# Opening of a hybrid two-block transformer kernel: filler matmuls on zeros, x through a diagonal of roots, two weight slots issued ahead of the vectors

## The reference, cut to what matters

```python
h_res = concatenate([meta, x], axis=1)                       # 272 rows x 1024
h = h_res * rsqrt(mean(h_res * h_res) + 1e-6) * pre_norm_g   # row by row
z = h @ w_in                                                 # 1024 x 7328
```

## Time and profile before

| | us |
|---|---|
| median of 3 runs | 927.73 |
| lowest and highest | 925.45, 928.86 |
| the profiled execution, its own time | 930.4 |
| its span in the profile | 928.7 |
| PE busy | 891.5 (96% of the span) |
| DVE busy | 607.8 |
| ACT busy | 438.3 |

### The profile page before, as it was taken

The page is one execution under the profiler, slowest core; times in us unless marked ns, Lnnn a source line. Parts: engine busy times, 40 slices in busy tenths (PEclk is TensorE's granted clock), DMA queues, the critical chain, the costliest instruction groups (busy, mean ns, idle before and its releaser), DMA issues.

```text
span 928.7 us, 14251 instructions
## 1 busy us (share of the span) xinstructions
PE 891.5 (96%) x6011; PEld 816.0 (88%) x6011; DVE 607.8 (65%) x851; ACT 438.3 (47%) x606; POOL 120.8 (13%) x109
## 2 busy tenths in 40 slices
PE   6999989999999999989999999989999899999994
PEld 5997989998888888779999988779988899999883
DVE  5996994786568745785555544676886755555446
ACT  5555453555645853434444443234564444444430
POOL 0333430121002101020000000023600200000002
PEclk9999998999999999989999999989999999999998
DMA  8663664663347552546666555446634565555641
GB/s 300 188 175 95 187 190 126 180 181 114 92 136 231 177 161 77 172 137 185 187 188 187 185 183 187 155 156 193 191 116 138 171 189 184 182 181 182 188 152 46
DMA packets 117801, 154.20 MB, mean 166 GB/s; under 512 B 5263, under 2 KB 95786, under 8 KB 117706
## 3 DMA queue, kind: packets, MB, share of 16 engines
q1 hardware_dynamic: 116266, 148.31, 52.7%
q0 software_dynamic: 1472, 4.98, 1.6%
HBM read 151.44 MB, written 1.05 MB: 164 GB/s over the span
## 4 chain that ended last, share of the span: by engine, by line
PE 88%; DVE 9%; DMA 2%; ACT 1%; issue 0%; DVEq 0%; SPq 0%
PE acc L527 25%; PE acc L528 25%; PE acc L529 25%; PE acc L565 3%; DVE w_lo L1471 2%; DVE conv L1617 1%; DVE y L1901 1%; PE misc L653 1%; DVE rs L1501 1%; PE misc L717 1%; DVE rs L1505 1%; DMA x<-in_x 1%; ACT w_hi L1073 1%; PE misc L898 1%; DVE stats L1888 1%; DVE y L1876 0%
## 5 line engine op out<-in xcount | busy, mean ns | idle before, releaser
L1471 DVE TENSOR_TENSOR w_lo<-staged,w_hi 128x1024 fp32r<-128x1024 f32 x274 | 340.1, 1251 | 226.2 <-ACT w_hi L1073 225.7
L1073 ACT CAST w_hi<-staged 128x1024 fp32r<-128x1024 f32 x274 | 285.2, 1045 | 239.4 <-DMA staged<-in_ffn_w_gu 71.5
L527 PE MATMUL acc<-x_hi,w_hi 128*128 128x256 f32 (+1 forms) x1296 | 368.1, 284 | 3.1 <-DVE m L1696 3.1
L528 PE MATMUL acc<-x_lo,w_hi 128*128 128x256 f32 (+1 forms) x1296 | 367.4, 283 | 0.0
L529 PE MATMUL acc<-x_hi,w_lo 128*128 128x256 f32 (+1 forms) x1296 | 364.6, 281 | 0.0
L527 PEld LDWEIGHTS acc<-x_hi,w_hi 128*128 128x128 f32 x1296 | 244.3, 188 | 5.5 <-DVE m L1696 3.3
L529 PEld LDWEIGHTS acc<-x_hi,w_lo 128*128 128x128 f32 x1296 | 246.6, 190 | 0.0
L528 PEld LDWEIGHTS acc<-x_lo,w_hi 128*128 128x128 f32 x1296 | 244.9, 189 | 0.4 <-issue 0.2
L2257 POOL TENSOR_TENSOR y<-y,gain 128x512 f32<-128x512 f32 x8 | 10.4, 1306 | 461.0 <-ACT y L1269 461.0
L527 PE MATMUL acc<-w_hi,h_hi 128*128 128x512 f32 x176 | 69.7, 396 | 0.3 <-DVE hidden L2051 0.3
L529 PE MATMUL acc<-w_hi,h_lo 128*128 128x512 f32 x176 | 69.6, 396 | 0.0
(11 more groups left out here) (368 smaller groups left out, 1126.2 us busy)
## 6 DMA issues: line engine op xcount, KB each, us to landing
staged<-in_ffn_w_gu SPq DMA_DIRECT2D x88, 512.0 KB, 3.5
staged<-in_w_in SPq DMA_DIRECT2D x58, 512.0 KB, 3.7
staged<-in_ffn_w_down SPq DMA_DIRECT2D x44, 512.0 KB, 3.5
staged<-in_gla_w_in SPq DMA_DIRECT2D x24, 512.0 KB, 3.6
staged<-in_moba_w_in SPq DMA_DIRECT2D x24, 512.0 KB, 3.9
staged<-in_w_o SPq DMA_DIRECT2D x8, 512.0 KB, 3.7
staged<-in_gla_w_out SPq DMA_DIRECT2D x8, 512.0 KB, 3.6
staged<-in_moba_w_out SPq DMA_DIRECT2D x8, 512.0 KB, 3.6
```

Source lines behind the costliest of these rows:

```text
L527: pe.matmul(dst, st_hi, mv_hi, start=start, stop=False)
L528: pe.matmul(dst, st_hi, mv_lo, start=False, stop=False)
L1073: nc.scalar.copy(hi, raw).then_inc(rounded, 1)
L1471: nc.vector.tensor_tensor(lo, raw, hi, ALU.subtract).then_inc(split, 1)
```

## The change

- **PE on zeros.** PE no longer waits for the identity before its first matmul. It does 10 filler matmuls on `w_gk`, cleared to zero by POOL (that memset moves ahead of the one of `w_pool`), then 5 instead of 4 fillers with the identity, and 3 instead of 1 behind the vectors.
- **Diagonals.** Instead of scaling the rows (one ACT and two DVE instructions of 1024 columns) DVE multiplies the identity by the roots: three diagonal matrices of 128 columns, in the same buffer that y used. PE then multiplies x by the diagonal, as a float32 matmul, where it transposed the scaled rows. DVE waits for `const_loaded` in addition.
- **Order of loads.** Slots 0 and 1 are issued right behind x and ahead of the 11 vector loads; slots 2 and 3 behind them. The meta rows and the identity are issued by ACT. ACT squares the meta rows first, then tile 0.

```diff
@@ SP @@
-            sp.dma_start(m_rows, d["meta_tokens"]).then_inc(s["meta_loaded"], 16)
-            sp.dma_start(const[:, 0:2 * P], d["constants"][:, 0:2 * P]).then_inc(s["const_loaded"], 16)
+            z_slots(0, 2)
             for name, n in VEC_ROWS:
...
-            z_slots(0, 4)
+            z_slots(2, 4)
@@ PE @@
+            pe.wait_ge(s["cleared"], 2)
+            for _ in range(10):
+                pe.matmul(open_bank("vec")[:, 0:2 * P], w_gk[:, 0:P], w_gk[:, 0:2 * P], start=True, stop=True)
             pe.wait_ge(s["const_loaded"], 16)
-            keep_awake(open_bank("vec"), 4)
+            keep_awake(open_bank("vec"), 5)
             pe.wait_ge(s["vec_loaded"], 16 * len(VEC_ROWS))
             filled(pe.transpose(open_bank("vec")[:, 0:VEC_N], vec_rows[0:VEC_N, :], ident[0:VEC_N, 0:VEC_N]), "vec")
-            keep_awake(open_bank("x0_0"), 1)
+            keep_awake(open_bank("x0_0"), 3)
             pe.wait_ge(s["normed"], 3)
...
-                    pe.transpose(b[:, 0:META], meta_h[:, cols], ident[0:META, 0:META])
+                    pe.matmul(b[:, 0:META], m_rows[:, cols], diag(2)[0:META, 0:META], start=True, stop=True)
                     for t in range(TILES):
-                        tr = pe.transpose(b[:, META + t * P:META + t * P + P], y[:, t, cols], ident)
-                    filled(tr, "x0_%d" % c)
+                        mm = pe.matmul(b[:, META + t * P:META + t * P + P], x[:, t, cols], diag(t), start=True, stop=True)
+                    filled(mm, "x0_%d" % c)
@@ ACT @@
+            act.dma_start(m_rows, d["meta_tokens"]).then_inc(s["meta_loaded"], 16)
+            act.dma_start(const[:, 0:2 * P], d["constants"][:, 0:2 * P]).then_inc(s["const_loaded"], 16)
+            act.wait_ge(s["cleared"], 1)
+            act.wait_ge(s["meta_loaded"], 16)
+            nc.scalar.activation(meta_h, m_rows, ACT.Square, accum_out=ssq[0:META, 1:2])
             act.wait_ge(s["x_loaded"], 16)
-            act.wait_ge(s["cleared"], 1)
-            nc.scalar.activation(y[:, 0, :], x[:, 0, :], ACT.Square, accum_out=ssq[:, 0:1])
-            act.wait_ge(s["meta_loaded"], 16)
-            nc.scalar.activation(meta_h, m_rows, ACT.Square, accum_out=ssq[0:META, 1:2]).then_inc(s["ssq0"], 1)
-
-            act.wait_ge(s["rstd0"], 1)
-            nc.scalar.activation(y[:, 0, :], x[:, 0, :], ACT.Copy, scale=rs[:, 1, 0:1]).then_inc(s["normed"], 1)
+            nc.scalar.activation(y[:, 0, :], x[:, 0, :], ACT.Square, accum_out=ssq[:, 0:1]).then_inc(s["ssq0"], 1)
@@ DVE @@
-            nc.vector.tensor_scalar(y[:, 1, :], x[:, 1, :], rs[:, 1, 2:3], None, ALU.mult).then_inc(s["normed"], 1)
-            nc.vector.tensor_scalar(meta_h, m_rows, rs[0:META, 1, 1:2], None, ALU.mult).then_inc(s["normed"], 1)
+            dve.wait_ge(s["const_loaded"], 16)
+            for i, rows in ((2, META), (0, P), (1, P)):
+                of = (0, 2, 1)[i]
+                nc.vector.tensor_scalar(diag(i)[0:rows, :], ident[0:rows, :], rs[0:rows, 1, of:of + 1], None,
+                                        ALU.mult).then_inc(s["normed"], 1)
@@ POOL @@
             nc.gpsimd.memset(ssq[:], 0.0).then_inc(s["cleared"], 1)
+            nc.gpsimd.memset(w_gk[:], 0.0).then_inc(s["cleared"], 1)
             nc.gpsimd.memset(w_pool[:], 0.0).then_inc(s["cleared"], 1)
-            nc.gpsimd.memset(w_gk[:], 0.0).then_inc(s["cleared"], 1)
```

More of the change, by code:

```diff
@@ L339, in hybrid_stack, with diag @@
         trig_k, trig_kh = conf_sq[0:ROPE, 0, :], conf_sq[0:ROPE, 1, :]
+        def diag(i):
+            return y[:, 1, i * P:i * P + P]
         kvq_rs = [scratch[:, i * 528:(i + 1) * 528] for i in range(3)]
@@ L441, in _, with z_slots @@
                 sp.dma_start(x[:, t, :], d["x"][0, t * P:t * P + P, :]).then_inc(s[name], 16)
-            sp.dma_start(m_rows, d["meta_tokens"]).then_inc(s["meta_loaded"], 16)
-            sp.dma_start(const[:, 0:2 * P], d["constants"][:, 0:2 * P]).then_inc(s["const_loaded"], 16)
+            w_in = d["w_in"][0]
+            def z_slots(lo, hi):
+                for sl in slots(lo, hi - lo):
+                    load(sl, k_half(w_in, sl.at % 2, Z_BLOCKS[sl.at // 2][1]))
+            z_slots(0, 2)
             for name, n in VEC_ROWS:
```

## The result

| us | before | after |
|---|---|---|
| median | 927.50 (6 runs) | 934.23 (6 runs) |
| lowest and highest | 925.45, 928.86 | 931.54, 935.11 |
| the profiled execution, its own time | 930.4 | 931.54 |

The ratio is 1.0065 with a 95% interval of 1.0049 to 1.0081: the kernel became 6.0 us slower (4.5 to 7.5). Forecast was +2.5, in a range of 926 to 933.5, so the direction of the likeliest case was right, its size was not, and the time lies above the range. The profiled execution of after is its fastest run and that of before lies above its slowest; their difference of 1.1 us is therefore not the effect.

The account below looks back on a forecast made before the run. Vector work before `normed` was taken to bound the opening until 12.38 us, then PE's unbroken stream. Start -0.5 plus eight banks +3.0 gave +2.5 us: 927.73 + 2.5 = 930.2, range 926 to 933.5.

Parts of the forecast that it names:

- the likeliest case: Whole kernel: first bank 0.5 us earlier, eight banks 3.0 us longer, so +2.5 us; chance 0.57.
- the start of the turning: Opening, ahead of PE's first bank: shorter DVE work lets it start at 11.9 instead of 12.38, 0.5 us earlier.
- The bank: PE's eight opening banks: matmuls with diagonals instead of transposes add 0.38 us each, 3.0 us together (1.8 to 4.2).
- the 0.06 for the weight loads: Within each opening bank on PE: weight loads not hidden at two changes of shape, 0 to 0.10 us, taken as 0.06.
- The rival of the factor of four: Opening banks: a tile's float32 matmul costs four times its transpose, +3.4 us more, 933.6; chance 0.10.
- One to one: From the opening to the kernel's end: PE's lateness or gain in the opening passes through in full.
- The rival of the swallowed delay: Around 140 us: PE's 3.1 us idle wait for m absorbs the delay, clock may stay up; 927.7 or 925; chance 0.17.
- The sum: Whole kernel: -0.5 + 3.0 = +2.5 us, from +0.9 to +4.5, on a median of 927.73.
- Roots come late: Opening: meta rows squared first delay the sums DVE needs, 0.6 late for 930.8 or 2.5 late for 932.7; chance 0.10.
- Zeros don't bring the clock up: Opening, PE: fillers on zeros leave the clock low or it falls again, start 4.6 us later, 935.3; chance 0.06.

Follow-up runs that it names:

- the run with the vectors first: Changed kernel with the 11 vector loads issued ahead of slots 0 and 1, meta rows and identity still issued by ACT: 932.3 us, ratio 1.0052.
- the run with fillers alone: Kernel before with ten more filler matmuls ahead of the first bank of transposes, nothing else changed: 932.17 us, ratio 1.0049.
- the execution with two slots first: Kernel before with only slots 0 and 1 issued ahead of the vector loads, one profiled execution: 933.31 us.
- the one with ACT issuing: Kernel before with four convolution taps moved behind the first sum m, meta rows and identity issued by ACT, meta rows squared first: 924.5 us, ratio 0.9971.
- with the taps moved: Kernel before with four of DVE's 31 convolution taps moved from ahead of the first sum m to behind it: 922.89 us, ratio 0.9947.

## Why the prediction was wrong

- **The step that failed is the start of the turning.** It put the last vector load at "about 6.4" and had it landed "by 10.9 at the latest if it takes as long as the whole of that", that is 4.5 us after its issue, as before. The issue was right (6.45). The landing was at 11.69, 5.24 after the issue, and in the other executions with two slots ahead of them the vectors took 4.70 to 5.59 us. I had taken the 4.5 us of before, where only the meta rows and the identity, 192 KB, stood between x and the vectors, as good with 1 MB directly before them on the same queue. The Trainium skill, "DMA: Bandwidth & Descriptors", section Queues, rings and completion order, says that each DMA engine consumes a queue's descriptors in ring order; the run with the vectors first fits it (issued 5.02, transposed at 10.02 without a wait, so landed within 5.0), but no run shows the order itself, and the later issue alone, 6.45 against 5.90, makes 0.55 of the lateness. Behind the late vectors stand the transpose and six filler instructions (1.30 us, four of the six are the change's), so the first bank came at 13.36. The likeliest case had left this tail out: even with a landing at 10.9 the transpose and the fillers end at about 12.6, later than the 12.4 that it gave as the latest; the landing 0.8 later makes the rest. PE's work before the vectors was sized well: the ten with the identity ended at 10.2, forecast 10.0 to 10.8. Forecast: first bank 0.5 earlier. Measured: 1.0 later. The error is 1.5 us, and the run with the vectors first gives back 1.5 at slot 2.
- **The diagonals as such were sized well**: 0.67 us for three (0.69 forecast), ready at 11.65 (11.9 forecast), and alone they bring the first bank forward by 0.5 to 0.6.
- **The bank was a little under-sized.** Forecast +0.38, measured 0.96 - 0.53 = +0.43, so 3.4 instead of 3.0 for eight. The two tiles bring 0.64 - 0.37 = 0.27, where the forecast had 0.22, and the 16-column product 0.16, the high end, where it had 0.10; the 0.06 for the weight loads is in these two and not beside them. The rival of the factor of four fell: a tile's float32 matmul takes 0.32 us in these banks and its transpose 0.18, less than a factor of two. The Trainium skill ("TensorE: Matmul & The Clock Gate", Terms) calls transpose mode 4 times faster for float32; this trace doesn't bear that out for this shape.
- **One to one held as far as the traces show it.** 4.3 us at slot 2, 4.3 at `kr_z`; the run with fillers alone lost 4.5 us of time for 4.4 of lateness. The rival of the swallowed delay fell: the wait for m stayed 3.0, for DVE's sum m itself came 4.2 later (143.24 against 139.05). What I had not seen is that the slow clock behind it belongs to some executions only. In the profiled execution of after it was absent, as that rival has it, with the gap still there; that is chance between executions and not a gain of the change, for the next profile of the same kernel has the fall.
- **The sum.** 1.0 + 3.4 = 4.4, against 4.31 measured at slot 2. The forecast had -0.5 + 3.0 = 2.5, its own upper end 4.5. So of the error against the measured 6.0, 1.5 us is the start, 0.4 the banks, and 1.6 has no cause that a run shows. That the likeliest case had the direction right owes nothing to the start, which it had with the wrong sign.
- **What remains** between 4.4 and the 6.0 of the ratio (6.7 by the medians) is open. It isn't the fall of the clock, for it stands at equal granted clock too, and it isn't made at the wait for m. It is near the edge of what these runs can tell: the ratio's interval begins at 4.5. Taken off the changed kernel one at a time, the order of loads gives back 1.3 us of time and the diagonals 4.3, together 5.6; the zeros, by one execution, nothing.
- The other two rivals. *Roots come late* fell: the meta rows landed by 4.38 and the sums were read at 7.86. *Zeros don't bring the clock up* fell too: durations of the 20 zeros lie between 792 ns and 379, and the fillers behind them run at 0.23. But in the one execution without them PE's clock was up by 13.75 all the same.

## What to carry to other kernels

Before you move large loads ahead of small ones, look for who waits for the small ones and what is queued behind that wait; a landing time in a trace is the time with what stood before it then. Replacing a scale and a transpose by one multiplication with a diagonal has to save more before the path than it adds on it: here it took 0.7 us off DVE, of which 0.6 reached PE, and laid 3.4 on PE, which sets the end. PE had a hole of 3 us at 140 us, often with a slow clock behind it; moving the DVE work that stood just before it was worth more (4.9 us by the ratio) than anything done to the opening.

## What the runs showed of the hardware

- When TensorE's clock reaches its high level (2.4 GHz) in the opening differs between executions: fillers of 379 ns by 14.5, but of 634 ns until 18.6 in the execution with two slots first and until 17.8 in the one with ACT issuing. In the latter it cost 2.7 us (3.2 less the 0.5 of the later start). Two executions of one kernel differ too: with the taps moved, the first bank's two tiles took 0.60 us in one and 0.37 in another. PE had been on fillers from 7.3 us in before and from 7.1 with ACT issuing, so the start of its work doesn't explain the difference. Its idle time ahead of the first bank was 0.2 us in before, 0.5 with ACT issuing, and 1.3 (ahead of the vectors) with two slots first; whether that is the reason, no run shows. The column of the granted clock reads 1.00 in those stretches all the same, so that here durations and counts have to be read.
- Whether the clock falls behind the 3 us without work at 140 us differs too: in the first profile of the changed kernel it did not, in its second it did, at a cost of 2.7 us (158.2 - 155.5 at `conv`).
- A float32 matmul of 16 partitions by 16 columns takes as much per instruction as its transpose, 0.16 us (0.32 / 2 and 0.16). In these banks the matmul instructions of 128 x 128 advance by 0.16 too (0.64 / 4), where a stream of that shape alone goes by 0.111. So few columns save nothing here; whether the change of shape or the weight load is what costs, no run separates.
